# Decoder block with product-key experts, one core: searches placed among projections, normed rows remade on DVE, gathers indexed from the table

## The chip, the cores and the metric

The kernel runs on one core of a Trainium2 chip. The metric is the device time of one execution in microseconds, median of several runs, lower is better.

## The reference

One decoder block over 1024 tokens of width 1024, float32. First RMSNorm, one projection into six parts of 512, stick-breaking attention with 8 heads on three of them, a gated causal convolution of three taps on the other three; both normed, projected by `w_out` and added to x. Then the part in which the change lies, a retrieval of experts (PEER), and a last RMSNorm:

```python
xn = rmsnorm(x, ffn_norm_g)
q = (xc @ wq).reshape(128, 8, 256)                      # xc: 128 tokens of xn
s1, s2 = q[..., :128] @ keys[0], q[..., 128:] @ keys[1]   # 128 keys each
v1, i1 = top_k(s1, 16); v2, i2 = top_k(s2, 16)
cand = v1[..., :, None] + v2[..., None, :]              # 256 pairs
best, pos = top_k(cand, 16); idx = cand_idx[pos]        # of 16384 experts
g = softmax(best)
w = g * gelu(xc . u_tab[idx])
x = x + sum over heads and k of w * v_tab[idx]
```

So each of 1024 tokens reads 8 x 16 = 128 experts, and of each a row of `u` and a row of `v`, 8 KB together.

## The kernel before

**Chunks, slots, groups.** The tokens are eight chunks of 128, one token to a partition. A chunk has 128 slots, one expert of every token each. A slot is one indirect DMA of 1 MB (L758): for each partition the row of `u` and `v` beside each other, into one of eight places of `ring`. Four slots (chunks 0 and 1) or two (the others) make a group. What a group goes through:

- POOL (L742 to L760) waits until the search has found the indices (`s_exp`) and DVE has freed the first place (`s_vd`), copies the group's indices from the table `idx` into `cur_idx` (L749), waits for the copy, and then issues one gather for each slot, after DVE (`s_vd`) and PE (`s_vp`) have freed the place.
- DVE, parts 0 and 1: for each slot the dot product of the u row with the token's normed row `xn` (L1158). ACT, part 1: gelu (L797). DVE, part 2: times the gate (L1167), and then it adds the weighted v rows to `acc` (L1178). ACT, part 2: a diagonal matrix of the weights (L801). PE, part 2: diagonal times v row into PSUM, the first 512 columns (L983) and in some groups the others too (L987). In "narrow" groups PE takes two of four slots, and DVE adds the whole row of the others.
- After a chunk's last group `final_sum` (L1419, L1421) adds PSUM and `acc`; `final_root` and `final_scale` norm the result, and SP stores it.

**Fronts.** What comes before the groups of a chunk is its front: norm, projections (L1017, L1021), attention, convolution, output projection, second norm (`norm_x2`, L1279), queries (L1100), scores of the keys (L1113), the best 16 of each half (`top_keys`, L1292 to L1305) and the search: `pair_sums` and `top_pairs` (L1325 to L1350), `gate_start` (L1357 to L1369), `look_up` (L1380 to L1395) and `experts` (L1406 to L1411) on DVE, with `gate_exp` and `spread` (L928, L936) on ACT. Fronts are made for batches of chunks, [0], [1, 2], [3, 4, 5] and [6, 7]. In batch 0 a search covers two of eight heads, later four. After `norm_x2` SP stores the new x and the normed rows in DRAM (`spill`, L660 and L661), and `load_chunk` (L678, L679) loads both into `xn` and `acc` before the chunk's groups.

**The order.** `timeline()` writes out one list of groups' parts and front steps, and every engine walks through its own share of it in order. First comes the front of batch 0; once its first search is done, one part of a group follows each further step. Then a batch's front is spread by costs among the groups of the chunks before it: batch 1 among those of chunk 0, batch 2 in chunks 1 and 2, batch 3 in chunks 3 to 5. Chunks 6 and 7 have no front beside them: their first and last 8 slots are written out, the 14 bodies between run as a loop with a register. In a loop the indices' place in `idx` depends on the register.

Four searches of batch 0 stand in its query phase, one after every four lists. They use `xn` and `acc` of the other parity as room (`big`), and `ocT` for the lists (`tk`), which batch 1's front overwrites; so ACT's `store_h` of batch 1 waits for the last of them.

## Time and profile before

| | |
|---|---|
| median of 3 runs | 3197.33 us (3192.45 to 3197.36) |
| the profiled execution: own time / span | 3201.8 / 3200.1 us |
| mean granted TensorE clock | 0.863 |
| first gather / last sum of chunk 0 | 124.6 / 632 us |
| last sums of chunks 1, 2, 5, 6, 7 | 1057, 1467, 2551, 2872, 3193 us |

The profile is of one execution, in microseconds from its first instruction. Busy time is what an engine spends in instructions; a wait is the idle time before an instruction, put down to what ended last. PEclk is the granted share of TensorE's full clock. The stretches in the rows below end at the last sums of chunks.

### The profile page before, as it was taken

The numbers are of one execution on the slowest core, as the hardware profiler recorded it, in microseconds if no ns is written. First come the engines' busy times: TensorE is split into PE (matmuls) and PEld (weight loads), VectorE is DVE, ScalarE is ACT, GpSimd is POOL, SyncE is SP. The second block draws the span as 40 slices with busy tenths as digits, with TensorE's granted clock in tenths as the row PEclk, the third lists the DMA queues.
The fourth block names the chain that finished last, engine by engine and source line by source line (L and its number), as shares of the span: only waits on it lengthen the run. The fifth ranks groups of instructions, "written<-read, shape, count | busy, mean of one in ns | idle before, by whom it ended". The sixth has DMA issues, their size and how long they took to land.

```text
span 3200.1 us, 28861 instructions
## 1 busy us (share of the span) xinstructions
PE 2377.9 (74%) x7332; PEld 1255.1 (39%) x7332; DVE 2499.8 (78%) x5544; ACT 996.5 (31%) x2273; POOL 1526.3 (48%) x1488
## 2 busy tenths in 40 slices
PE   8759868588888897777787888777677756555555
PEld 7538546245545454223563444344333311111111
DVE  1676759879888789887677888879977788888887
ACT  2131521332465411234116747412122221112111
POOL 0132333333443433455444545544455567776775
PEclk9879879889999898888988989878898987777777
DMA  6879789889988999999999999999999999999998
GB/s 244 312 296 385 292 344 397 337 331 402 374 333 323 373 419 338 351 382 380 419 419 396 380 356 406 388 420 412 381 397 407 418 422 422 422 422 422 422 422 346
DMA packets 184026, 1209.11 MB, mean 378 GB/s; under 512 B 20560, under 2 KB 20560, under 8 KB 52432
## 3 DMA queue, kind: packets, MB, share of 16 engines
q0 software_dynamic: 147456, 1073.81, 83.1%
q1 hardware_dynamic: 36432, 133.73, 10.9%
q8 instruction: 55, 0.90, 0.1%
q14 instruction: 83, 0.68, 0.1%
HBM read 1194.87 MB, written 12.58 MB: 377 GB/s over the span
## 4 chain that ended last, share of the span: by engine, by line
DVE 32%; DMA 26%; PE 23%; ACT 11%; issue 6%; POOL 2%; POOLq 0%; DVEq 0%; SPq 0%; ACTq 0%
DMA ring<-in_uv,cur_idx 24%; DVE ring L1158 13%; PE vacc L983 8%; DVE acc L1178 7%; PE bank L1021 5%; ACT L776 3%; PE bank L1089 3%; POOL ring L758 2%; ACT g_ge L797 2%; ACT diag L801 1%; PE bank L1017 1%; PE o_ps L987 1%; DVE lt L1295 1%; DMA xn_scratch<-xb 1%; DVE g_w L1167 1%
## 5 line engine op out<-in xcount | busy, mean ns | idle before, releaser
L983 PE MATMUL vacc<-ring,diag 128*128 128x512 f32 x1872 | 1180.7, 759 | 751.7 <-ACT diag L801 751.5
L758 POOL DMA_INDIRECT ring<-in_uv,cur_idx x1024 | 1197.2, 1169 | 1017.3 <-PE vacc L983 459.3
L1158 DVE CUSTOM_DVE_ANT_0 ring<-ring,xn 128x1024 f32<-128x1024 f32 x1024 | 1229.5, 1221 | 246.8 <-DMA ring<-in_uv,cur_idx 244.4
L983 PEld LDWEIGHTS vacc<-ring,diag 128*128 128x128 f32 x1872 | 395.6, 229 | 1404.9 <-ACT diag L801 1054.1
L1178 DVE SCALAR_TENSOR_TENSOR acc<-ring,g_w,acc 128x512 f32<-128x512 f32 (+1 forms) x854 | 689.1, 807 | 40.5 <-DVE g_w L1167 0.3
L749 POOL COPY cur_idx<-idx 128x2 uint32<-128x2 uint32 (+2 forms) x448 | 327.2, 730 | 631.5 <-DVE acc L1178 489.6
L797 ACT ACTIVATE g_ge<-dots 128x2 f32<-128x2 f32 (+1 forms) x448 | 91.2, 204 | 1656.2 <-DVE dots L1158 1655.5
L801 ACT ACTIVATE diag<-ident,g_w 128x128 f32<-128x128 f32 x936 | 322.1, 393 | 124.3 <-DVE g_w L1167 124.2
L1021 PE MATMUL bank<-hT,wpool 128*128 128x256 f32 (+2 forms) x1280 | 289.8, 385 | 3.3 <-ACT hT L831 3.3
L1021 PEld LDWEIGHTS bank<-hT,wpool 128*128 128x128 f32 x1280 | 223.6, 196 | 78.1 <-issue 19.5
L776 ACT ACT_TABLE_LOAD x187 | 239.9, 1283 | 4.1 <-PEq L1447 0.8
L1100 PE MATMUL bank<-hT,wpool 128*128 128x256 f32 (+2 forms) x1024 | 240.0, 391 | 1.4 <-ACT hT L913 1.4
L1167 DVE TENSOR_TENSOR g_w<-g_ge,gate 128x2 f32<-128x2 f32 (+1 forms) x448 | 72.0, 161 | 200.8 <-ACT g_ge L797 200.6
L1100 PEld LDWEIGHTS bank<-hT,wpool 128*128 128x128 f32 x1024 | 180.5, 200 | 47.8 <-issue 3.4
L987 PE MATMUL o_ps<-ring,diag 128*128 128x512 f32 x340 | 193.0, 652 | 0.0
L987 PEld LDWEIGHTS o_ps<-ring,diag 128*128 128x128 f32 x340 | 72.1, 212 | 95.4 <-issue 95.4
L1032 PEld LDWEIGHTS bank<-qT,kT 64*128 64x128 f32 x576 | 71.0, 194 | 50.9 <-issue 43.3
L1032 PE MATMUL bank<-qT,kT 64*128 64x128 f32 x576 | 84.0, 291 | 1.2 <-ACT ab L882 1.2
L1158 DVE DVE_READ_ACCUMULATOR2_ANT dots<- 128x1 f32 x1024 | 84.9, 83 | 0.0
L1066 PEld LDWEIGHTS o_ps<-ab,vN 128*64 128x64 f32 x576 | 61.9, 138 | 45.0 <-issue 41.2
L1066 PE MATMUL o_ps<-ab,vN 128*64 128x128 f32 x576 | 78.7, 282 | 0.0
L1050 PE MATMUL bank<-lb,neg_tri 128*128 128x512 f32 x144 | 78.4, 627 | 0.0
(143 smaller groups left out, 1602.6 us busy)
## 6 DMA issues: line engine op xcount, KB each, us to landing
wpool<-in_w_in SPq DMA_DIRECT2D x96, 512.0 KB, 7.9
wpool<-in_peer_wq SPq DMA_DIRECT2D x64, 512.0 KB, 8.7
wpool<-in_w_out SPq DMA_DIRECT2D x32, 512.0 KB, 7.9
ring<-in_uv,cur_idx POOLq DMA_INDIRECT x1024, 11.6
xb<-in_x SPq DMA_DIRECT2D x15, 512.0 KB, 8.3
x_scratch<-xb SPq DMA_DIRECT2D x8, 512.0 KB, 10.1
xn_scratch<-xb SPq DMA_DIRECT2D x8, 512.0 KB, 12.5
xn<-xn_scratch SPq DMA_DIRECT2D x8, 512.0 KB, 8.5
```

The lines of the kernel that those rows point to most:

```text
L749: nc.gpsimd.tensor_copy(cur_idx[:, sl], idx[:, c % KEEP, bass.ds(i * RING + q * group_of(c), group_of(c))])\
L758: nc.gpsimd.indirect_dma_start(ring[:, s, :], None, uv, bass.IndirectOffsetOnAxis(ap=cur_idx[:, s:s + 1], axis=0))\
L776: nc.scalar.preload_act_table_set(name)
L797: nc.scalar.activation(g_ge[:, sl], dots[:, sl], ACT.Gelu_apprx_tanh).then_inc(s_gge, 1)
L801: nc.scalar.activation(diag[:, q * group_of(c) + s, :], ident[:, :], ACT.Copy, scale=g_w[:, q * group_of(c) + s:q * group_of(c) + s + 1]). ...
L983: ins = nc.tensor.matmul(vacc[:, :], diag[:, q * group_of(c) + s, :], ring[:, q * group_of(c) + s, D:D + PE_COLS], start=first and s == 0, ...
L987: ins = nc.tensor.matmul(o_ps[:, :], diag[:, q * group_of(c) + s, :], ring[:, q * group_of(c) + s, D + PE_COLS:2 * D], start=first_wide an ...
L1021: ins = nc.tensor.matmul(b[:, 0:T], w[:, k * P:(k + 1) * P], hT[:, k, 0:T], start=k == 0, stop=k == KD - 1)
L1032: ins = nc.tensor.matmul(b[:, i * P:(i + 1) * P], kT[rows, i, kb * P:(kb + 1) * P], qT[rows, i, span(c)], start=i == 0, stop=False, skip_g ...
L1100: ins = nc.tensor.matmul(b[:, 0:T], w[:, k * P:(k + 1) * P], hT[:, k, 0:T], start=k == 0, stop=k == KD - 1)
L1158: ins = nc.vector.tensor_tensor_reduce(out=ring[:, s, 0:D], in0=ring[:, s, 0:D], in1=xn[:, c % 2, :], scale=1.0, scalar=0.0, op0=ALU.mult, ...
L1178: nc.vector.scalar_tensor_tensor(out=acc[:, c % 2, lo:D], in0=ring[:, s, D + lo:2 * D], scalar=g_w[:, s:s + 1], in1=acc[:, c % 2, lo:D], o ...
```

## The change

**Searches.** In batch 0's query phase only the first search stays. `own_places` puts the other three into chunk 0's groups: for heads 2, 4 and 6 the pairs go behind part 2 of groups 3, 5 and 7, `gate_start` behind part 0 of the next group, `look_up` behind its part 2, and `experts` behind part 0 of the group after it. The lists of chunk 0 move from `ocT` to `lists_own`, and `store_h` of batch 1 no longer waits for the searches. Batch 1's front begins after group 2 instead of group 3.

**Normed rows.** `spill` stores only x, `load_chunk` loads only `acc`, and a new step `norm_chunk` on DVE makes the chunk's normed rows in `xn` from `acc`, the row's root (now kept per chunk in `root2`) and the gain. `load_chunk` 0 moves ahead of the first query; `norm_chunk` stands after the first search for chunk 0, and for the others near the end of the chunk before.

**Indices.** In written-out groups the gather takes its indices from a column of `idx`, and POOL copies none; it waits for `s_exp`, and for each slot for `s_vd` and `s_vp`. In loops the copy stays.

```diff
-        if bi == 0 and (t + 1) % (2 * hs) == 0:
-            search(at, k + 4, chunks[0], t // 2 + 1 - hs)
+        if bi == 0 and t + 1 == 2 * hs:
+            search(at, k + 4, chunks[0], 0)
...
+def own_places():
+    hs, places = heads_per_search(0), {}
+    for h in range(hs, PH, hs):
+        g = OWN_FIRST + h - hs
+        for i, step in enumerate(own_search(h)):
+            places.setdefault((g + (i + 1) // 2, 0 if i % 2 else 2), []).append(step)
+    return places
...
     for step in front_steps(0):
+        if ("pe", "query", 0, 0) in step:
+            out.append(("front", "sp", "load_chunk", 0))
...
                 if not known:
-                    out.append(("front", "sp", "load_chunk", 0))
+                    out.append(("front", "dve", "norm_chunk", 0))
...
                     out.append(("group", c, g, part))
+                    if c == 0:
+                        for step in own.pop((g, part), []):
+                            out += phases(step)
...
+                if g == groups_of(c) * 31 // 32:
+                    out.append(("front", "dve", "norm_chunk", c + 1))
...
-                    sp.dma_start(xn_d[c], xb[:, 1, :]).then_inc(s_spx, 16)
...
-                    sp.wait_ge(s_spx, 32 * (c + 1))
-                    sp.dma_start(xn[:, c % 2, :], xn_d[c]).then_inc(s_chunk[c % 2], 16)
+                    sp.wait_ge(s_spx, 16 * (c + 1))
                     sp.dma_start(acc[:, c % 2, :], x2_d[c]).then_inc(s_chunk[c % 2], 16)
...
-                if not very_first:
+                copied = not isinstance(i, int)
+                if copied:
                     pool.wait_ge(s_vd, used + 1)
-                sl = slice(q * group_of(c), (q + 1) * group_of(c))
-                nc.gpsimd.tensor_copy(cur_idx[:, sl], idx[:, c % KEEP, bass.ds(i * RING + q * group_of(c), group_of(c))])\
-                    .then_inc(s_idx, 1)
-                pool.wait_ge(s_idx, group_no(c, i, q) + 1)
+                    sl = slice(q * group_of(c), (q + 1) * group_of(c))
+                    nc.gpsimd.tensor_copy(cur_idx[:, sl],
+                                          idx[:, c % KEEP, bass.ds(i * RING + q * group_of(c), group_of(c))])\
+                        .then_inc(s_idx, 1)
+                    pool.wait_ge(s_idx, copies(c, i, q) + 1)
...
-                    nc.gpsimd.indirect_dma_start(ring[:, s, :], None, uv,
-                                                 bass.IndirectOffsetOnAxis(ap=cur_idx[:, s:s + 1], axis=0))\
+                    row = cur_idx[:, s:s + 1] if copied else idx[:, c % KEEP, i * RING + s:i * RING + s + 1]
+                    nc.gpsimd.indirect_dma_start(ring[:, s, :], None, uv, bass.IndirectOffsetOnAxis(ap=row, axis=0))\
                         .then_inc(s_gat[s], 16)
...
-                    if bi > 0:
+                    if bi > 1:
                         act.wait_ge(s_exp, found([e for e in BATCHES[bi - 1] if e not in LATE][-1], PH - 1))
...
                     if c >= KEEP:
-                        dve.wait_ge(s_idx, groups_ahead(c - KEEP + 1))
+                        dve.wait_ge(s_fsum, c - KEEP + 1)
...
+                elif name == "norm_chunk":
+                    c, = args
+                    dve.wait_ge(s_chunk[c % 2], 16 * (c // 2 + 1))
+                    if c == 1:
+                        dve.wait_ge(s_exp, found(0, PH - 1))
+                    if c >= 2:
+                        dve.wait_ge(s_fsq, c - 1)
+                    nc.vector.scalar_tensor_tensor(out=xn[:, c % 2, :], in0=acc[:, c % 2, :], scalar=root2[:, c:c + 1],
+                                                   in1=ffn_gain[:, :], op0=ALU.mult, op1=ALU.mult).then_inc(s_xnc, 1)
```

How the order moves, at three places. DVE in the query phase, from the end of the first search, before (the names are output<-inputs; `ocT` and `bank` rows are a step of `top_keys`):

```order
L1411 TENSOR_TENSOR gate<-srch,gs 128x32
L1325 TENSOR_TENSOR xn<-ocT 128x2x128
L1326 TENSOR_TENSOR xn<-ocT 128x2x8
L1337 MAX srch<-xn 128x8 x2
L1340 MATCH_REPLACE acc<-srch,xn 128x136 x2
L1344 MAX_INDEX srch<-srch,xn 128x8 x2
L1347 MAX srch<-acc 128x8 x2
L1350 MAX_INDEX srch<-srch,acc 128x8 x2
L1292 MAX ocT<-bank 128x8
```

and in the changed kernel, whose line numbers stand 41 higher here:

```order
L1452 TENSOR_TENSOR gate<-srch,gs 128x32
L1333 MAX lists_own<-bank 128x8
L1336 MATCH_REPLACE lt<-lists_own,bank 128x128
L1340 MAX_INDEX lists_own<-lists_own,bank 128x8
L1343 MAX lists_own<-lt 128x8
L1346 MAX_INDEX lists_own<-lists_own,lt 128x8
L1462 SCALAR_TENSOR_TENSOR xn<-acc,root,ffn_gain 128x1024
```

The pairs of the second search are gone from here; the lists follow at once, and `norm_chunk` 0 after one list.

DVE in the changed kernel at groups 4 and 5, where batch 1's projections run (ISA rows are dot products):

```order
L1208 TENSOR_TENSOR g_w<-g_ge,gate 128x4
L1219 SCALAR_TENSOR_TENSOR acc<-ring,g_w,acc 128x512 x4
L1421 TENSOR_TENSOR xn<-acc,iota 128x1024
L1425 TENSOR_TENSOR acc<-xn,srch 128x1024
L1432 TENSOR_TENSOR xn<-acc 128x512
L1432 TENSOR_TENSOR acc<-xn 128x256
L1432 TENSOR_TENSOR xn<-acc 128x128
L1436 TENSOR_TENSOR srch<-xn 128x64
L1199 ISA ring,dots<-ring,xn 128x1024
```

The look-up of the second search now stands between group 4's additions and group 5's dot products.

POOL from the first gather on, with the semaphores it waits for, before:

```order
L749 COPY cur_idx<-idx 128x4 [waits s_exp]
L758 DMA ring<-in_uv,cur_idx 128x2048 [waits s_idx]
L758 DMA ring<-in_uv,cur_idx 128x2048 x3
L749 COPY cur_idx<-idx 128x4 [waits s_exp]
L758 DMA ring<-in_uv,cur_idx 128x2048 [waits s_idx]
L758 DMA ring<-in_uv,cur_idx 128x2048 x3
L749 COPY cur_idx<-idx 128x4 [waits s_vd,s_exp]
L758 DMA ring<-in_uv,cur_idx 128x2048 [waits s_idx,s_vd,s_vp]
L758 DMA ring<-in_uv,cur_idx 128x2048 [waits s_vd,s_vp] x3
```

and changed:

```order
L800 DMA ring<-in_uv,idx 128x2048 [waits s_exp]
L800 DMA ring<-in_uv,idx 128x2048 x3
L800 DMA ring<-in_uv,idx 128x2048 [waits s_exp]
L800 DMA ring<-in_uv,idx 128x2048 x3
L800 DMA ring<-in_uv,idx 128x2048 [waits s_exp,s_vd,s_vp]
L800 DMA ring<-in_uv,idx 128x2048 [waits s_vd,s_vp] x3
```

The copies and the waits for them are gone; the first gather of a group waits for both engines itself.

## Rows read from the trace of the kernel before

**Rows 1.** The page: busy time of each engine (share of the span) x instructions.
```profile
PE 2377.9 (74%) x7332; PEld 1255.1 (39%) x7332; DVE 2499.8 (78%) x5544; ACT 996.5 (31%) x2273; POOL 1526.3 (48%) x1488
```

**Rows 2.** Busy time by stretch: us, engines (x instructions), PEclk, DMA share, GB/s.
```profile
222.00:305.00 83.00, 82.45 (x416) 69.81 (x417) 51.80 (x87) 12.06 (x37) 26.57 (x28) 1.00 0.98 387
...
222.00:632.00 410.00, 335.67 (x1307) 224.47 (x1308) 304.22 (x744) 113.76 (x240) 141.23 (x136) 0.90 0.90 352
...
124.00:1467.00 1343.00, 1061.98 (x3618) 611.81 (x3616) 1092.49 (x2688) 445.01 (x918) 532.04 (x523) 0.89 0.91 356
1467.00:2551.00 1084.00, 842.47 (x2468) 436.21 (x2468) 851.86 (x1819) 398.71 (x888) 544.92 (x576) 0.88 0.98 399
2551.00:2872.00 321.00, 182.73 (x256) 57.24 (x256) 260.10 (x451) 61.65 (x198) 228.58 (x192) 0.77 1.01 422
```

**Rows 3.** Waits (us in total, times, longest): 124 to 1467 us, then 1467 to 2551.
```profile
POOL ring L758 <- PE vacc L983: 231.1, 81, 12.8
...
DVE ring L1158 <- DMA ring<-in_uv,cur_idx: 75.6, 45, 5.1
...
DVE ring L1158 <- DMA ring<-in_uv,cur_idx: 121.9, 109, 3.1
```

**Rows 4.** DVE in order of time, 152 to 173 us: start, us, operation.
```profile
152.75 0.18 DVE L1406 TENSOR_REDUCE gs<-srch 128x2 f32<-128x32 f32 x1
...
153.46 0.42 DVE L1325 TENSOR_TENSOR xn<-ocT 128x256 f32<-128x256 f32 x1
...
156.84 0.30 DVE L1292 MAX8 ocT<-bank 128x8 f32<-128x128 f32 x1
...
169.66 0.68 DVE L1380 TENSOR_TENSOR xn<-acc,iota 128x1024 bf16<-128x1024 bf16 x1
...
172.41 0.30 DVE L1292 MAX8 ocT<-bank 128x8 f32<-128x128 f32 x1
```

**Rows 5.** DVE, ACT and PE in order of time, from 134.99 us.
```profile
134.99 1.22 DVE L1158 CUSTOM_DVE_ANT_0 ring<-ring,xn 128x1024 f32<-128x1024 f32 x1 [5.08 <-DMA ring<-in_uv,cur_idx]
...
197.53 1.06 ACT L816 ACTIVATE xb<-xb 128x1024 f32<-128x1024 f32 x1
...
209.38 1.06 ACT L816 ACTIVATE xb<-xb 128x1024 f32<-128x1024 f32 x1 [4.96 <-DMA xb<-in_x]
...
214.47 5.30 PE L983 MATMUL vacc<-ring,diag 128*128 128x512 f32 x8 [11.91 <-ACT diag L801]
```

**Rows 6.** The page: costliest groups, DVE's dot products and additions.
```profile
L1158 DVE CUSTOM_DVE_ANT_0 ring<-ring,xn 128x1024 f32<-128x1024 f32 x1024 | 1229.5, 1221 | 246.8 <-DMA ring<-in_uv,cur_idx 244.4
...
L1178 DVE SCALAR_TENSOR_TENSOR acc<-ring,g_w,acc 128x512 f32<-128x512 f32 (+1 forms) x854 | 689.1, 807 | 40.5 <-DVE g_w L1167 0.3
```

**Rows 7.** PE in order of time, 222 us: the first projection of batch 1.
```profile
222.55 2.64 PE L1021 MATMUL bank<-hT,wpool 128*128 128x256 f32 x11 [1.91 <-ACT hT L831]
```

**Rows 8.** POOL in order of time, 1240 us: copy and the two gathers behind it.
```profile
1240.34 0.69 POOL L749 COPY cur_idx<-idx 128x2 uint32<-128x2 uint32 x1 [0.43 <-DVE acc L1178]
1241.97 0.96 POOL L758 DMA_INDIRECT ring<-in_uv,cur_idx  x1 [0.93 <-PE vacc L983]
1243.24 0.94 POOL L758 DMA_INDIRECT ring<-in_uv,cur_idx  x1 [0.30 <-issue]
```

**Rows 9.** Copies and gathers on POOL: duration ns min/median/max.
```profile
L749 POOL COPY cur_idx<-idx x448: 182/691/1284, 123.5 to 3170.9; 128x2 uint32<-128x2 uint32 x91, 128x2 uint32 x37, 128x4 uint32<-128x4 uint32 x22
...
L758 POOL DMA_INDIRECT ring<-in_uv,cur_idx x1024: 932/1010/1999, 124.6 to 3174.8; - x171
```

**Rows 10.** The page: DMA issues x count, KB each, median us to landing.
```profile
x_scratch<-xb SPq DMA_DIRECT2D x8, 512.0 KB, 10.1
xn_scratch<-xb SPq DMA_DIRECT2D x8, 512.0 KB, 12.5
xn<-xn_scratch SPq DMA_DIRECT2D x8, 512.0 KB, 8.5
```

**Rows 11.** The multiplication that makes the normed rows: duration ns min/median/max.
```profile
L1279 DVE SCALAR_TENSOR_TENSOR xb<-xb,st,ffn_gain x8: 1279/1280/1284, 91.3 to 2089.0; 128x1024 f32<-128x1024 f32 x8
```

More of the change, by code:

```diff
@@ L43 @@
 EARLY_PARTS = 1
+OWN_FIRST = 3
 PARTS = 3
@@ L200, in front_steps, with own_search, at @@
     return [steps[i] for i in sorted(steps)]
+def own_search(h):
+    steps = {}
+    def at(k, eng, *phase):
+        steps.setdefault(k, []).append((eng, *phase))
+    search(at, 0, 0, h)
+    return [steps[i] for i in sorted(steps)]
+def own_places():
[5 more added lines that the diff above has]
+    return places
 COST = {"gate_h": 0.9, "conv_taps": 1.6, "att_soft": 0.8, "att_carry": 0.6, "gain_mix": 1.2, "add_mix": 1.3,
@@ L452, in build @@
         st = sb("st", [P, 16])
+        root2 = sb("root2", [P, CHUNKS])
         dots = sb("dots", [P, RING])
@@ L584, in diags_ahead, with copies @@
             return slot_no(c, i, q) - sum(group_of(e[0]) // 2 for e in narrow if e < (c, g))
+        looped = [c for kind, c, first, count in (ph for ph in line if ph[0] == "body") if count > 1]
+        def copies(c, i, q):
+            ahead = sum((BODIES - 2) * lap_of(k) for k in looped[:looped.index(c)])
+            return (i - 1) * lap_of(c) + (ahead + q)
         def gather_line(eng_group, eng_front, me):
```

20 lines of the change are left out of this document (12 added, 8 removed).

## The prediction, made before the changed kernel ran

> **What bounds the kernel now.** I read the page first, for the shares of the engines [rows 1]: DVE is busy 78% of the span, PE 74%. No engine is full over the whole span, so the page alone doesn't tell what bounds it. The busy time by stretch does [rows 2]. In the last two chunks, where only loops run, DMA moves 422 GB/s at a share of 1.01 while DVE has a fifth of its time free: bytes bound that part, and I take 422 GB/s as what DMA can give. From 1467 to 2551 us it is 399 GB/s at a share of 0.98, almost as full. From 124 to 1467 us it is 356 GB/s at 0.91, with DVE busy 1092.5 of 1343 us. There nothing is full; the stretch is bound by latency, by engines that work in order and wait for one another. So a saved wait can pay before 1467 us, and after it mainly saved bytes. Then I read the waits, to see what of DVE's idle time hangs on gathers: 75.6 us in 45 waits before 1467 us and 121.9 us in 109 waits after it [rows 3]. The rest of DVE's idle time hangs on PE and ACT.
>
> **Step 1, own searches (-13 us).** The change takes the last three searches of chunk 0 out of the query phase and puts them among batch 1's projections. One such search costs DVE 0.71 us for the experts, 3.38 us for pair sums and top pairs (152.75 to 153.46 to 156.84), and 2.75 us for the look-up (169.66 to 172.41) [rows 4]; the start of the gates is as many small operations as the experts, so another 0.7. That is 7.5 us, and 22.5 us for three. None of it goes away; the question is where it stands.
>
> How much sooner do the projections begin? The first dot product waits for its gather until 134.99, and batch 1's first norm starts on ACT at 197.53 [rows 5]. Of the DVE work between the two, the change takes out 22.5 us of searches, except the 3.4 us of pairs that already ran before 134.99, so 19; and it takes out one group of four slots (turn_h(1) now follows group 2, it followed group 3), four dot products of 1.22 us and four additions of 0.75 to 0.81 us, about 8 us [rows 6]. DVE is nearly full there, so the norm starts 27 us sooner. The second norm keeps its 11.85 us behind the first (its x has to be loaded). In the trace of before, its transposes then stand behind group 4's product, 5.30 us on PE [rows 5]; in the new order they stand ahead of group 3's. So the projections start not 27 but 32 us sooner, at about 190 instead of 222.55 [rows 7].
>
> What has to be done afterwards is more, by the same searches and one group. The searches fall into the projections, where PE is busy 82.45 of 83 us at full clock and DVE 51.8 [rows 2]: 31 us free for 22.5 us of searches, though not always at the right moment. I let 4 us of them through. The one group costs what a group costs in the rest of this stage: 410 us for 26 to 27 groups, 15 us. So 32 - 15 - 4 = 13 us gained. The ends: if the additional 30.5 us of DVE work is done at DVE's present share of that stage (304.22 of 410, 0.74 [rows 2]) it takes 41 us, 9 us more than the head start; if all of it finds a gap, the whole 32 us stay. I take 13 because the projections, the nearest rows, have the gap in the very place.
>
> **Step 2, POOL's copies (-18 us).** 336 of the 448 copies go; the 112 in the loops stay. A copy takes 0.69 us and the gather behind it starts 0.93 us after its end, where gathers behind each other stand 0.30 us apart [rows 8]: a group's gathers can leave 0.69 + 0.93 - 0.30 = 1.32 us earlier if the copy is what they wait for. Often it isn't: the copy waits only for DVE, the gather also for PE's product, and where PE is last (230 us of POOL's waits before 1467 us name it, [rows 3]) the copy is hidden already. What an earlier gather is worth is bounded by the waits of DVE for gathers. Before 1467 us: 45 waits of at most 1.32 us, 59 us; at the low end nothing, if PE is last each time. I take a fifth, 12 us, since many of the 45 also wait behind weights in the DMA queues. From 1467 to 2551 us, DMA's share leaves 2% of 1084 us, 22 us [rows 2]; I take 6. Together 18, between 0 and 81.
>
> Here a rule speaks against a part of this. The copy takes 182 ns at its fastest and 691 in the median [rows 9], and it mostly starts as DVE's first addition of a group ends and the second, which reads two operands from SBUF, begins. The gather too varies, from 932 to 1999 ns [rows 9]. 
>
> **Step 3, no normed rows in DRAM (-10 us).** Eight stores and eight loads of 512 KB go [rows 10], 8.4 MB, at 422 GB/s 20 us. That is the far end; the near end is 0, if they all lie where DMA has room. They are spread over all stages; the ones behind 1467 us lie where DMA is at a share of 0.98 and more [rows 2], so I take half, 10. In it is a shorter wait for the spill: the store of the normed rows lands 12.5 us after its issue in the median, and the next x, the squares and the keys wait for it. SP now waits for the spill of chunk 0 (a median of 10.1 us to landing) before it issues the last eight weight tiles of the queries; the tiles are prefetched eight deep, and DVE, which takes the results, is behind by then. I cost it at nothing; uncovered it would be at most those 10 us.
>
> **Step 4, remaking them (+4 us).** DVE gets eight multiplications of 128x1024, as long as the ones that make the rows today, 1.28 us [rows 11], 10.2 us in all. The load of each is issued several groups before, so none should wait. Three are in the stages before 1467 us, where DVE's work is paid: 4 us. The others lie where DMA is full and cost nothing (at the far end all 10). Two more table loads on ACT, and lists of chunk 0 in another buffer, I cost at nothing: ACT is busy 31% [rows 1].
>
> **Sum.** -13 - 18 - 10 + 4 = -37 us. The profiled execution took 3201.8 us around a span of 3200.1; it stands 4.5 us above the median of the runs, 3197.33. So 3165 for such an execution and 3160 us against the median.
>
> **The rivals.**
> (a) *DMA sets the pace anyway.* Waits saved before 1467 us are lost again at the chunk's ends, and only bytes count: 5 to 10 us, about 3190. For it: shares of 0.9 and more nearly everywhere. Against it: 356 GB/s instead of 422 in the first 1343 us. Chance 0.14; half of it lies within 0.2%, which is 6 us and about what a measurement of this kernel can tell from no change.
> (b) *The wait for DVE passes to the gather.* Of the 1.32 us, 0.69 - 0.18 = 0.51 go back; step 2 gives 18 x 0.81 / 1.32 = 11 us, and the time is 3167. For it: the 691 against 182 ns. Against it: gathers behind DVE's additions also come at 0.93 us. Chance 0.12.
> (c) *The copies and idle gaps pay fully.* Steps 1 and 2 near their far ends, -28 and -40, step 3 -15, step 4 +4: 3118. For it: every chunk before 1467 us is a chain of waits. Chance 0.14.
> (d) *Slower: the searches stop the projections.* DVE works in order; a search between two parts of a group holds the dot products, then ACT's gelu, then PE's products, which stand in PE's queue ahead of the next projection. It decides against the change as soon as less than about half of the searches finds a gap while the head start is spent. Price +9 us by the far end of step 1 and +10 of step 4; if at the same time PE is last for every gather (step 2 gives 0) and bytes give 5: 3197 + 14 = 3211. Chance 0.09. Against it: 31 us free on DVE in the projections.
> My forecast, 3140 to 3180, has the remaining 0.51.
>
> **How the numbers follow.** The time is that of the forecast, 3160. The range reaches up to rival (a), 3193, and down to (c), 3118; outside lie (d) and pieces of (a) and (c), some 0.2. Faster by over 0.2%: 0.51 + 0.12 + 0.14 + half of (a) = 0.84; within 0.2%: 0.08 with a little of (d); slower 0.08.
>
> **What would show it.** Right: the first projection (L1021 with 128x256) at about 190 us, chunk 0's last sum some 13 to 30 us sooner than 632; DVE's share in the projections up from 0.62 to near 0.9; no copy before 2550 us; gathers 0.30 us behind each other also at a group's start, of 0.93 to 1.2 us each; DMA 8.4 MB less, its rate before 1467 us up from 356 GB/s; the last two chunks at 321 us as now. Wrong: first projection later than 200; PE idle between projections with DVE in a search; gathers at a group's start of 1.5 us and more (b); every stage shorter only by its bytes (a); a wait of DVE for the rows of a chunk.

## The result, and the profile after

The changed kernel takes 3168.05 us (median of 4 runs, 3166.28 to 3171.32) where the kernel before, measured beside it, takes 3196.52 (4 runs, 3192.45 to 3197.36): a ratio of 0.9914, 95% interval 0.9898 to 0.9931. That is 28 us faster. The forecast was 37 us faster, 3160, with a range of 3118 to 3193.

The profiled execution took 3166.99 us around a span of 3164.9; before it was 3201.8 around 3200.1. So the profiled pair shows some 7 us more than the medians do, and every difference between single profiles below carries a few us of that kind.

The page of the changed kernel, busy time and DMA packets [rows 1 and 10 answer to it]:

```profile
PE 2361.8 (75%) x7332; PEld 1248.4 (39%) x7332; DVE 2507.5 (79%) x5552; ACT 998.0 (32%) x2275; POOL 1337.3 (42%) x1152
...
DMA packets 181717, 1200.68 MB, mean 379 GB/s; under 512 B 20304, under 2 KB 20304, under 8 KB 50128
```

1200.68 MB are 8.4 MB less than before, as the forecast's third step said. DVE has 8 us more work than before (2507.5 us, it had 2499.8 [rows 1]) and 35 us less to do it in.

Where the time went shows in the end of each chunk (us from the span's start), read from the records of both traces as the start of DVE's last sum, which adds PE's columns from `vacc` to `acc`:

| chunk | 0 | 1 | 2 | 3 | 4 | 5 | 6 | 7 |
|---|---|---|---|---|---|---|---|---|
| before, end | 632 | 1057 | 1467 | 1841 | 2213 | 2551 | 2872 | 3193 |
| after, end | 603 | 1029 | 1438 | 1811 | 2181 | 2519 | 2838 | 3158 |
| before, length | 632.1 | 424.8 | 409.8 | 374.1 | 371.9 | 338.6 | 321.2 | 320.8 |
| after, length | 603.3 | 425.4 | 409.7 | 372.4 | 370.2 | 337.7 | 319.3 | 320.2 |

28.8 us are gone by the end of chunk 0, and 6.3 in the seven chunks after it. Some of the 28.8 is the profiled execution of before being late there: in four kernels below that leave the searches where they were and differ from before in other things (idx_only, split_waits, store_kept, two_copies) chunk 0 ends at 625 to 629. So 22 to 26 us are nearer to what the change takes off chunk 0. The same stretches as in [rows 2], bounded by the chunks' new ends (columns: us, engines busy with their instructions, granted clock as a share of 2.4 GHz, DMA share, GB/s):

```profile
190.00:273.00 83.00, 83.00 (x396) 67.92 (x395) 71.16 (x191) 22.44 (x48) 27.27 (x22) 0.99 0.94 369
...
222.00:603.00 381.00, 310.52 (x1178) 200.92 (x1177) 312.06 (x798) 116.32 (x239) 126.17 (x107) 0.89 0.90 360
124.00:1438.00 1314.00, 1052.23 (x3621) 605.42 (x3619) 1095.47 (x2691) 445.39 (x919) 454.15 (x391) 0.90 0.91 360
1438.00:2519.00 1081.00, 836.32 (x2468) 435.50 (x2468) 856.13 (x1824) 399.81 (x889) 442.38 (x385) 0.89 0.98 398
2519.00:2838.00 319.00, 181.65 (x256) 56.67 (x256) 260.58 (x452) 61.63 (x198) 221.70 (x184) 0.76 1.01 422
```

The first line is the stretch of batch 1's projections. PE is as full as before, and DVE is busy 71.16 of 83 us where it was busy 51.80 [rows 2]. The last three lines are shorter than those of [rows 2] by 29, 3 and 2 us, and apart from POOL's the engines' busy times are nearly the same: before chunk 3 the rate is 360 GB/s instead of 356, from there to chunk 5's end 398 instead of 399. POOL is busy 78 us less before 1438 us, and 103 us less from there to 2519. What that did to the gathers the next views show.

The head start, in the order of time of ACT and of PE (start, us, operation, in brackets the idle time before it and its releaser, that is, what ended last before it); the answers to [rows 5] and [rows 7]:

```profile
170.09 1.06 ACT L857 ACTIVATE xb<-xb 128x1024 f32<-128x1024 f32 x1
```

PE in order of time, from the second norm's transposes to the first projection:

```profile
185.22 1.72 PE L1043 MATMUL bank<-ident,xb 128*128 128x128 f32 x8 [4.66 <-ACT xb L860]
189.08 5.31 PE L1024 MATMUL vacc<-ring,diag 128*128 128x512 f32 x8 [2.15 <-ACT diag L842]
194.22 5.99 PE L1062 MATMUL bank<-hT,wpool 128*128 128x256 f32 x27
```

The norm of batch 1 starts at 170.09 instead of 197.53 us, 27.4 sooner; the first projection at 194.22 instead of 222.55, 28.3 sooner. The second norm came at 182.22, 12.1 us behind the first. Its transposes do stand ahead of a group's product now, at 185.22, but group 3's product (5.31 us) still stands between them and the first projection.

The waits that the second step hung on, before chunk 2's end (us in total, times, longest); [rows 3] answers:

```profile
DVE ring L1199 <- DMA ring<-in_uv,idx: 70.3, 45, 5.9
```

And from there to chunk 5's end:

```profile
DVE ring L1199 <- DMA ring<-in_uv,idx: 116.4, 105, 2.6
```

DVE waited for gathers 75.6 us in 45 waits before and waits 70.3 in 45 now; behind chunk 2 it was 121.9 us in 109, now 116.4 in 105. The copies' removal was to shrink these.

How a gather at a group's start stands to PE, in rows of PE and of POOL. They answer to [rows 8]. PE's product of two slots (four matmuls) there begins at 1239.91:

```profile
1239.91 1.98 PE L983 MATMUL vacc<-ring,diag 128*128 128x512 f32 x4 [2.31 <-ACT diag L801]
```

Its second matmul, the one that frees the first place, ends at 1241.03, and the copy ends at 1241.03 too. The gather starts at 1241.97, 2.06 us behind the product's start. Then the changed kernel, PE, DVE and POOL together:

```profile
1206.65 1.91 PE L1024 MATMUL vacc<-ring,diag 128*128 128x512 f32 x4
...
1207.57 1.22 DVE L1199 CUSTOM_DVE_ANT_0 ring<-ring,xn 128x1024 f32<-128x1024 f32 x1
...
1208.50 1.10 POOL L800 DMA_INDIRECT ring<-in_uv,idx  x1 [5.39 <-PE vacc L1024]
...
1210.86 1.98 PE L1024 MATMUL vacc<-ring,diag 128*128 128x512 f32 x4 [2.31 <-ACT diag L842]
...
1212.79 0.94 POOL L800 DMA_INDIRECT ring<-in_uv,idx  x1 [1.95 <-PE vacc L1024]
```

Without a copy the gather comes 1.85 and 1.93 us after the product's start, with the copy 2.06. In these groups the copy costs 0.1 to 0.2 us and not 1.32, since the gather waits for the product in both kernels.

How it is over all groups can be read from the records of both traces. In both kernels the first gather of a group never starts sooner than 0.80 us behind the end of the matmul that frees its place; in the changed kernel it starts just then in most groups, and in the kernel before in half of them. In the latter no first gather starts sooner than 0.93 us behind the end of its copy either. So one can ask for each of the 318 groups of chunks 0 to 5 that wait for a place how much later the first gather left than PE and the gather before it allow:

| first gathers of a group that left late: how many, us in all | before | changed | idx_only | two_copies |
|---|---|---|---|---|
| chunks 0 to 2, of 126 groups | 49, 25 | 3, 4 | 3, 4 | 73, 70 |
| chunks 3 to 5, of 192 groups | 101, 67 | 6, 6 | 6, 6 | 149, 169 |

(idx_only and two_copies are experiments below: the kernel before without the copies, and with a second one.) Before, 150 of 318 first gathers left late, by 0.59 us in the median and 92 us in all, and 138 of them started within 0.96 us behind their copy. Without copies it is 9, by 9 us. So the copies cost the gathers 82 us in all; three quarters of that lie in chunks 3 to 5, where DMA's share is 0.98.

### The profile page after: what moved, and what is told of

Same layout as the page of the kernel before. It is cut to its first block, busy times and chain, and to the rows that moved or that the text cites. A ratio compares the mean times of both kernels' runs of the same rounds, so it can differ in the third digit from the quotient of the medians.

```text
span 3164.9 us, 28192 instructions
## 1 busy us (share of the span) xinstructions
PE 2361.8 (75%) x7332; PEld 1248.4 (39%) x7332; DVE 2507.5 (79%) x5552; ACT 998.0 (32%) x2275; POOL 1337.3 (42%) x1152
## 2 busy tenths in 40 slices
DMA packets 181717, 1200.68 MB, mean 379 GB/s; under 512 B 20304, under 2 KB 20304, under 8 KB 50128
## 4 chain that ended last, share of the span: by engine, by line
DVE 30%; DMA 28%; PE 23%; ACT 11%; issue 6%; POOL 2%; POOLq 0%; DVEq 0%; ACTq 0%; SPq 0%
DMA ring<-in_uv,idx 15%; DVE ring L1199 13%; DMA ring<-in_uv,cur_idx 11%; PE vacc L1024 9%; DVE acc L1219 7%; PE bank L1062 5%; ACT L817 4%; PE bank L1130 3%; ACT g_ge L838 1%; ACT diag L842 1%; POOL ring L800 1%; PE bank L1058 1%; DVE lt L1336 1%; DVE g_w L1208 1%; DMA x_scratch<-xb 1%
## 5 line engine op out<-in xcount | busy, mean ns | idle before, releaser
L800 POOL DMA_INDIRECT ring<-in_uv,idx x800 | 927.2, 1159 | 1646.5 <-PE vacc L1024 854.7
L800 POOL DMA_INDIRECT ring<-in_uv,cur_idx x224 | 286.4, 1279 | 145.0 <-POOL cur_idx L789 80.1
L789 POOL COPY cur_idx<-idx 128x2 uint32 x112 | 121.7, 1087 | 11.8 <-DVE acc L1219 11.2
```

The lines of the kernel that those rows point to most:

```text
L800: nc.gpsimd.indirect_dma_start(ring[:, s, :], None, uv, bass.IndirectOffsetOnAxis(ap=row, axis=0))\
```

## The experiments

All 12 kernels have medians beside the kernel before, on the same chip; its medians there were 3195.88 to 3197.74 us. First the three parts of the change, each alone, and the change without one of them.

### Own searches alone: own_only

The kernel before with the three searches of chunk 0 moved among batch 1's projections, their lists in a buffer of their own and ACT's `store_h` of batch 1 no longer waiting for them, and nothing else. What the dropped wait is worth without the move wasn't measured.

```diff
+OWN_FIRST = 3
-        if bi == 0 and (t + 1) % (2 * hs) == 0:
-            search(at, k + 4, chunks[0], t // 2 + 1 - hs)
+        if bi == 0 and t + 1 == 2 * hs:
+            search(at, k + 4, chunks[0], 0)
+    own = own_places()
                     out.append(("group", c, g, part))
+                    if c == 0:
+                        for step in own.pop((g, part), []):
+                            out += phases(step)
```

> The kernel before with the searches moved and nothing else: POOL's copies and the normed rows in DRAM stay. Theory O (the gain is that of the searches; in the changed kernel chunk 0's stage ends 28.8 us sooner and the seven others together only 6.3): chunk 0's last sum at 603 to 608 us instead of 632, ratio to before 0.991 to 0.993. Theory C (searches bring the 13 us that the prediction gave them, the copies the other 15 in chunk 0): last sum at 617 to 621, ratio 0.995 to 0.997.

Measured: 3179.66 us (3173.36 to 3184.39, 6 runs) beside 3197.6, ratio 0.9941 (0.9921 to 0.996): 18 us. Chunk 0 ends at 607 instead of 632 (or of 625 to 629, above). This part carries most of the gain. By the interval it is 13 to 25 us, so the forecast's 13 lies at its lower end. The ratio lies between those of the two theories and is clear of neither; the stage's end fits theory O.

### Indices straight from the table alone: idx_only

```diff
-                nc.gpsimd.tensor_copy(cur_idx[:, sl], idx...)\
-                    .then_inc(s_idx, 1)
-                pool.wait_ge(s_idx, group_no(c, i, q) + 1)
+                copied = not isinstance(i, int)
+                if copied:
...
+                    row = cur_idx[:, s:s + 1] if copied else idx[:, c % KEEP, i * RING + s:i * RING + s + 1]
```

> The kernel before with gathers that take their indices from the table in written-out groups, and nothing else. Theory O: nothing, ratio 0.999 to 1.001, every stage within 2 us, since a gather waits for PE's product or starts 0.9 us after its release with and without a copy. Theory C: chunk 0's last sum 10 to 15 us sooner, ratio 0.993 to 0.997.

Measured: 3196.65 us (3190.67 to 3202.98, 12 runs) beside 3197.6, ratio 0.9996 (0.9983 to 1.0008). The 320 copies of chunks 0 to 5 are gone and the time doesn't move. The stages of its profiled execution, the fastest of the twelve, aren't all within 2 us of before (chunk 0 ends at 625, chunk 4 takes 366 us instead of 372), so theory O holds for the time and not for every stage. A first view of why is what released the gathers. The trace of the kernel before, POOL's idle time ahead of its gathers from 124 to 2551 us, by releaser (us in total, times):

```profile
L758 POOL DMA_INDIRECT ring<-in_uv,cur_idx x775: 932/962/1999, 124.6 to 2549.7; - x194
its engine sat idle before it (us, times) until:
  PE vacc L983: 426.7, 203
  issue: 180.9, 419
  PE o_ps L987: 101.3, 47
  DVE acc L1178: 79.8, 45
  POOL cur_idx L749: 38.0, 41
```

And idx_only in the same stretch:

```profile
  PE vacc L992: 846.4, 206
  DVE acc L1187: 286.7, 47
  PE o_ps L996: 186.6, 74
```

Before, the view names the copy 41 times and PE 250 times (203 and 47). Without copies PE is named 280 times and DVE 47, and their idle times are longer by what the copy had cut out of them. But the 41 is too low a count of the groups that a copy held up. The view names whatever ended last before the gather, and that is often PE's product for the next place, not for the one that this gather takes. Measured from the matmul that frees the place, it was some 140 groups (table above).

So the gathers did leave sooner in idx_only, by 82 us in all, and the kernel's time doesn't show it: the gain is 1 us, by the interval between 5 us faster and 3 slower. What is known of the reason is where the 82 us lie, 61 of them in chunks 3 to 5, in which DMA has 2% of its time free, and 21 in chunks 0 to 2. DVE's waits for gathers from 124 to 2551 us were 197.5 us before and are 193.2 here. Why 21 us of sooner gathers in the first chunks bring nothing that can be seen, no run shows.

### Normed rows remade alone: norm_only

```diff
-                    sp.dma_start(xn_d[c], xb[:, 1, :]).then_inc(s_spx, 16)
-                    sp.dma_start(xn[:, c % 2, :], xn_d[c]).then_inc(s_chunk[c % 2], 16)
+                elif name == "norm_chunk":
...
+                    nc.vector.scalar_tensor_tensor(out=xn[:, c % 2, :], in0=acc[:, c % 2, :], scalar=root2[:, c:c + 1],
+                                                   in1=ffn_gain[:, :], op0=ALU.mult, op1=ALU.mult).then_inc(s_xnc, 1)
```

> The kernel before with the normed rows remade on DVE and not stored, and nothing else. Theory O: only the bytes count, and only where DMA is full (chunks 2 to 7, some 12 of 16 transfers of 1.3 us at most): ratio 0.997 to 0.999. Rival: DVE's 10 us cancel them, ratio 0.9995 to 1.002, with chunks 0 to 2 slower by 1.3 us each.

Measured: 3186.66 us (3180.63 to 3191.32, 11 runs) beside 3197.6, ratio 0.9968 (0.9956 to 0.9979): 11 us. Steps 3 and 4 together were forecast at 6, and theory O's range is just missed on the fast side.

### The change with the copies put back: own_norm

```diff
-                copied = not isinstance(i, int)
-                if copied:
+                if not very_first:
...
+                                                  bass.IndirectOffsetOnAxis(ap=cur_idx[:, s:s + 1], axis=0))\
```

> The changed kernel with POOL's copies back in every group. Theory O: as fast as the changed kernel, ratio to before 0.990 to 0.993, chunk 0's last sum at 603 to 606. Theory C: chunk 0's last sum at 613 or later and ratio 0.994 or more.

Measured: 3172.31 us (3168.7 to 3174.76, 6 runs) beside 3197.6, ratio 0.9921 (0.9904 to 0.9938): 25 us, where the change has 28 (0.9914, 0.9898 to 0.9931). The two intervals overlap almost wholly. The ratio is theory O's; chunk 0 ends at 608, between the two theories' places. The parts add up within their spread: 18 and 11 are 29, beside 25 for both together. The copies are worth 1 us by idx_only and 3 by this pair, where 18 were forecast; neither is clear of zero.

### A second copy for each group: two_copies

If taking a copy away gives nothing, does a second one cost anything? The kernel before with one more copy ahead of the first, waited for.

```diff
+                if isinstance(i, int):
+                    more[0] += 1
+                    nc.gpsimd.tensor_copy(spare_idx[:, sl], idx...).then_inc(s_idx2, 1)
+                    pool.wait_ge(s_idx2, more[0])
                 nc.gpsimd.tensor_copy(cur_idx[:, sl], idx...)
```

> The kernel before with a second copy of a group's indices on POOL ahead of the first one, waited for, in the written-out groups: some 1.6 us more between DVE's release and the gather. Theory H (one copy is hidden because PE's product ends later than the copy, by little): the two no longer fit, a gather leaves about 1.5 us later in most groups, and chunks 0 to 5 lose part of it: ratio 1.002 to 1.02. Rival (gathers' departure has slack everywhere in these stages): 1.000 to 1.002.

Measured: 3203.63 us (3195.26 to 3207.19, 12 runs) beside 3197.74, ratio 1.002 (1.0008 to 1.0033): 6 us slower. POOL in order of time shows two groups. In both the gather starts 0.93 us behind the second copy's end, though the view names PE in one of them:

```profile
1253.38 0.69 POOL L755 COPY spare_idx<-idx 128x2 uint32<-128x2 uint32 x1 [3.82 <-DVE acc L1187]
1254.13 0.18 POOL L758 COPY cur_idx<-idx 128x2 uint32<-128x2 uint32 x1
1255.24 0.96 POOL L767 DMA_INDIRECT ring<-in_uv,cur_idx  x1 [0.93 <-PE vacc L992]
...
1261.49 0.69 POOL L755 COPY spare_idx<-idx 128x2 uint32<-128x2 uint32 x1 [4.04 <-DVE acc L1187]
1262.24 1.07 POOL L758 COPY cur_idx<-idx 128x2 uint32<-128x2 uint32 x1
1264.25 0.96 POOL L767 DMA_INDIRECT ring<-in_uv,cur_idx  x1 [0.93 <-POOL cur_idx L758]
```

By the table above 222 of 318 groups now leave later than PE allows, instead of 150, by 240 us in all instead of 92. (The view by releasers has 111 gathers named with a copy, instead of 41, and is too low in the same way.) So 148 us of later gathers cost 6 us, by the interval 3 to 11. Theory H expected 1.5 us more in most groups, and the mean is 0.5. At the same price the first copy's 82 us would be worth 3 us, which idx_only's interval and own_norm's 3 us allow. Whether the first copy costs nothing or those few us can't be told; that it costs 18 can be excluded.

### Which part of the moved searches pays: own_old_places and searches_apart

own_only does two things. It takes searches out of the time before the first projections and puts them into it; and the front steps of batch 1 start one group earlier. own_old_places keeps the first and undoes the second.

```diff
+    while early < 11:
+        out.append(("group", 0, *chunk0[early]))
+        early += 1
     own = own_places()
```

> own_only with batch 1's front started where the kernel before starts it (behind part 1 of group 3), so that every front step stands behind the same group part as before, and only the three searches are elsewhere. In own_only chunk 0 gains 8 us at group 5 and again 12 us between groups 17 and 18, where the kernel before stands 27 us. Theory G (the searches in the projections' gaps are the gain): this kernel keeps both parts, chunk 0's last sum at 605 to 612, ratio to before 0.993 to 0.996. Theory P (the second part is one of places: in own_only the output projection of chunk 2 stands elsewhere between the groups when its x is late): group 18's interval stays 25 to 27 us, last sum at 618 to 626, ratio 0.996 to 0.998.

Measured: 3181.15 us (3172.18 to 3190.2, 6 runs) beside 3197.74, ratio 0.9955 (0.9943 to 0.9967): 17 us, beside own_only's 18. The profiled execution was the fastest of the six, so its stages flatter it. The earlier front shows no worth of its own here; what pays is where the searches stand. The first projection came at 207.65 us:

```profile
207.65 7.17 PE L1051 MATMUL bank<-hT,wpool 128*128 128x256 f32 x32 [1.88 <-ACT hT L861]
```

That is 11.8 us later than own_only's 195.81, and yet the end is the same within the spread; more of the groups stand ahead of the front and are done by then. Here a head start of the projections and groups already done trade one for one (early_five, below, gets more out of a head start than this).

searches_apart moves the three searches of the changed kernel to the groups 3, 9 and 15, so that the later two stand behind the projections.

```diff
-        g = OWN_FIRST + h - hs
+        g = OWN_FIRST + (h - hs) * 3
```

> The changed kernel with its three searches behind groups 3, 9 and 15 instead of 3, 5 and 7: two of them in the attention, where DVE is fuller and PE emptier. Theory G (the gaps of the projections hide them): chunk 0's last sum 5 to 12 us later than 603, ratio to before 0.9935 to 0.996. Theory P: within 3 us of 603, ratio 0.990 to 0.993.

Measured: 3173.29 us (3167.24 to 3176.52, 5 runs) beside 3197.74, ratio 0.9922 (0.9909 to 0.9935); the change has 3168.05. Chunk 0 ends at 613 instead of 603. Its projections, 190 to 273 us:

```profile
190.00:273.00 83.00, 83.00 (x398) 68.02 (x397) 59.37 (x123) 14.24 (x38) 25.95 (x22) 0.99 0.95 370
```

DVE is busy 59.37 us here, and 71.16 in the changed kernel. Two searches that miss this gap cost some 5 us by the medians and 10 by the profiled chunk 0; 15 us of DVE work was moved. That would put the gap's worth at a third to two thirds of the work put in it. But the intervals of the two ratios overlap widely: chunk 0's end fits theory G, the ratio fits theory P, and the cost of the other places isn't proved.

### Bytes or waits in the remade rows: split_waits and store_kept

The kernel before had one semaphore for both stores of a spill, so the load of the next x waited for the second store too, without need. split_waits gives the second store a semaphore of its own and keeps all bytes.

```diff
+        s_spn = sem("s_spn")
-                    sp.dma_start(xn_d[c], xb[:, 1, :]).then_inc(s_spx, 16)
+                    sp.dma_start(xn_d[c], xb[:, 1, :]).then_inc(s_spn, 16)
...
-                        act.wait_ge(s_spx, 32 * c)
+                        act.wait_ge(s_spn, 16 * c)
```

> The kernel before with a semaphore of its own for the store of the normed rows: the next load of x waits only for the store of x, the next squares only for the store of the normed rows; both stores and both loads stay, all bytes too. Theory W (remaking the rows gains by the wait behind the second store, which ends 12.0 us after its issue where the store of x alone ends 8.7 us after): group 18 comes 2 to 8 us sooner as in norm_only (8.4), ratio 0.997 to 0.999. Theory B (it gains by its bytes): nothing, 0.9995 to 1.0005.

Measured: 3197.8 us (3191.67 to 3210.37, 12 runs) beside 3197.74, ratio 1.0003 (0.9992 to 1.0014). The load of x was issued 8.2 us behind the store instead of 12.1, and nothing came of it.

store_kept is norm_only (rows remade, none loaded) with the store of the normed rows put back, read by nobody.

```diff
                     sp.dma_start(x2_d[c], xb[:, 0, :]).then_inc(s_spx, 16)
+                    sp.dma_start(xn_d[c], xb[:, 1, :]).then_inc(s_spn, 16)
```

> The kernel before with the remade normed rows, and with the store of the normed rows to DRAM put back (its load is not): the rows in DRAM are read by nobody, the square of the next chunk waits for it with a semaphore of its own, the next x load for the store of x alone. norm_only took 10.9 us off (3186.66 beside 3197.6), split_waits (waits parted, bytes kept) nothing. Theory bytes of the store (4 MB that pass on the DMA rings in the stretch in which x_scratch is stored and x is loaded again, chunk 0's group 18 among it): nearly all of norm_only's gain is gone, 3194 to 3199, and the 27 us between groups 17 and 18 stay over 22. Theory load (the 4 MB read again, at the start of each chunk, are what counted) or theory wait: the gain stays, 3185 to 3190.

Measured: 3193.06 us (3186.99 to 3208.39, 12 runs) beside 3195.88, ratio 0.9989 (0.9974 to 1.0004). Of norm_only's 11 us about 3 are left, and these are not clear of zero. So dropping the load, with the remaking on DVE paid, was worth little, and dropping the store some 8, between the two theories and nearer to that of the store's bytes. The two ratios are 0.0021 apart and their intervals just touch, so the 8 is rough. ACT's wait for the last store, in the spill of chunk 1 (395 to 440 us; us in total, times, longest), shows one way in which it costs. The kernel before:

```profile
ACT xb L890 <- DMA xn_scratch<-xb: 7.7, 1, 7.7
```

norm_only:

```profile
ACT xb L895 <- DMA x_scratch<-xb: 4.0, 1, 4.0
```

store_kept:

```profile
ACT xb L900 <- DMA xn_scratch<-xb: 7.5, 1, 7.5
```

`square_mix` on ACT overwrites the normed rows, so it waits until they are stored. Between the `g_w` steps of groups 17 and 18 of chunk 0, where this spill lies, the kernels need 26.8 us (before), 22.0 (split_waits), 22.1 (store_kept) and 18.2 (norm_only). The step from 22 to 18 may be that wait's 3.5 us; the one from 26.8 to 22 isn't a result of any of the edits, as idx_only, which doesn't touch the spill, has 22.2 as well. Chunk 0 of the profiled execution of before was slow in this place. That is where some of the profiled pair's 35 us, against 28 by the medians, may come from.

### Could it be better: early_five, own_four, five_and_four

The groups ahead of the front of batch 1 are limited to five parts instead of what the finished searches allow, so that the front begins sooner; or the searches of chunk 0 stand one group later, behind groups 4, 6 and 8 instead of 3, 5 and 7 (the text on own_four below names other groups).

```diff
-                if chunk0[early][0] < known:
+                if chunk0[early][0] < known and early < 5:
```
```diff
-OWN_FIRST = 3
+OWN_FIRST = 4
```

> The changed kernel with at most five parts of chunk 0's groups written ahead of the front steps of batch 1, so that they begin sooner. Theory A (the gaps of the first projections are the only place in chunk 0 where DVE's searches hide; everything before them is paced by the DMA rings and by the norm of batch 1): the norm of batch 1 at ACT at 160 or sooner instead of 170, the first projection 5 to 10 us sooner than 194, time 3160 to 3166 beside 3168.05. Rival B (gathers pause while the front steps come first, the pause is not made good): 3168 to 3175.

> The changed kernel with each search of batch 1 one group later (behind groups 4, 5, 6 and not 3, 4, 5). Theory A (a search costs nothing as long as it lies in the projections' stretch, 190 to 273 us): within 3 us of 3168.05, chunk 0 ends at 601 to 607. Rival B (the place behind group 3 is just where DVE waits, one later runs into the sums of groups): 3172 to 3176, chunk 0 ends at 608 or later.

> The changed kernel with both moves: at most five parts ahead of the front steps of batch 1, and each search one group later. early_five measured 3160.38 us, own_four 3166.64 beside 3168.05 for the change. Theory (the two gains are separate and real): 3157 to 3161, under early_five's median. Rival (own_four's 1.4 us is the spread between executions, early_five's 7.7 is real): 3160 to 3164, same as early_five within its spread. Rival (early_five's median is luck as well, as its profiled execution shows chunk 0 ending at 604 beside 603): 3165 to 3170.

Measured: early_five 3160.38 us (3157.84 to 3162.44, 4 runs) beside 3195.88, ratio 0.9883 (0.9859 to 0.9906); own_four 3166.64 (3164.56 to 3168.93, 4 runs), ratio 0.9901 (0.9878 to 0.9924); both edits 3160.86 (3156.31 to 3167.37, 5 runs) beside 3196.72, ratio 0.9892 (0.9878 to 0.9906). The changed kernel had 3168.05, 0.9914 (0.9898 to 0.9931), beside other runs of before. The ratios' intervals overlap, so the 7 us between it and early_five aren't proved, but two kernels with that edit came out at the same 3160 to 3161. own_four can't be told from the change. early_five's PE in order of time:

```profile
185.43 7.17 PE L1062 MATMUL bank<-hT,wpool 128*128 128x256 f32 x32 [1.89 <-ACT hT L872]
192.44 3.60 PE L1024 MATMUL vacc<-ring,diag 128*128 128x512 f32 x8
```

The first projection is 8.8 us sooner than in the changed kernel, with the product that stood ahead of it (189.08 above) now behind it. That speaks against the one-for-one trade of own_old_places; the spread of that kernel's six runs, 18 us, leaves room for both. Where the 7 us show up isn't settled: in the profiled executions chunk 0 ends at 604 in early_five and at 596 in five_and_four beside 603, and early_five's chunk 4 takes 365.6 us beside 370.2, a difference that own_norm (367.2) and own_old_places (366.0) show as well, though their edits don't touch that chunk. early_five is the best version found: faster than before by 1.2% (0.9 to 1.4).

## Why the prediction was right, and where it was wrong

**What bounds the kernel.** Right as far as it went. The last two chunks stay at 422 GB/s and about 320 us, as forecast. From chunk 3 to 5 DMA's share of 0.98 stayed, and no gain from POOL can be seen there, though 61 of the 67 us by which first gathers were late there are gone. "Latency" before 1467 us was too coarse a word: it didn't say whose.

**Step 1, own searches, -13.** The mechanism was right and the size came out too small: own_only gained 18 us (13 to 25). The norm was forecast 27 us sooner and came 27.4 sooner. The projections were forecast 32 sooner, at 190, and came 28.3 sooner, at 194.22, since I read the order as if group 3's product had moved behind the first projection; it hadn't. That term was 4 us too good. "I let 4 us of them through" and "the one group costs 15 us" were then too dear. With 28 us of head start and 18 of gain, the two together cost 10 us, not 19. own_old_places suggests why the second hurts so little: with the groups ahead put back to their old number the time was the same within the spread (17 us gained), so a group that stands behind the front's start costs about what it gives. DVE's share in the projections went from 0.62 to 0.86, near the 0.9 named. Putting two searches elsewhere (searches_apart) cost 5 us, which isn't clear of the spread.

**Step 2, POOL's copies, -18.** Wrong. idx_only gave 1 us, within its interval nothing, and the change with the copies back lost 3 of 28, with intervals that overlap. Two readings failed. The first is the size of what a copy holds up: "a group's gathers can leave 0.69 + 0.93 - 0.30 = 1.32 us earlier if the copy is what they wait for". PE's product was there almost as late. The copy held up some 140 of 318 groups, and all copies together 82 us: 0.26 us for a group in the mean. In [rows 8] itself it was 0.13 us, with PE's matmul and the copy both ending at 1241.03; most of the 0.93 us behind the copy is also there behind a matmul (0.80 us at 1208.50 and 1212.79 above, without a copy).

The second and larger one is the worth of a sooner gather. The forecast took a fifth of 45 waits of 1.32 us before chunk 2's end, and 6 us behind it, from DVE's waits for gathers [rows 3]. The gathers left 82 us sooner in all in idx_only, and neither the time nor DVE's waits moved with it (75.6 to 70.3 and 121.9 to 116.4 in the changed kernel). From chunk 3 on this is where DMA was read as nearly full, and the 6 us there had no other ground than the 2% left. For the first three chunks the cause stays open.

**Rival (b), the wait for DVE passes to the gather.** Its time, 3167, is nearly the measured one; that is luck, since 0.51 us did not pass. The median over all gathers of chunks 0 to 5 fell from 962 to 938 ns:

```profile
L800 POOL DMA_INDIRECT ring<-in_uv,idx x776: 932/938/2139, 124.7 to 2518.8; - x194
```

That of a group's first gather, which the copy stood before, rose from 1.00 to 1.09 us, its mean from 1.18 to 1.19. All 768 gathers of chunks 0 to 5 together take 13 us more than before (887.6 and 874.6 us); 0.51 us for each of 320 groups would be 163. But the wait that (b) builds on is real, for gathers as well as for copies, and was there before the change. The 0.69 us of a copy that begins beside DVE's additions is what the rule of the Trainium skill, page "SBUF — State Buffer", section "SBUF: two separate sides", would have. This case's traces agree: in the kernel before, 374 copies began while DVE was in a dot product or an addition, which both read two operands from SBUF, and all 374 ended within 0.1 us of its end; the other 74 took 0.19 us in the median. How gathers wait is in the section on the hardware.

**Steps 3 and 4, the rows, -10 and +4.** norm_only gained 11 us where the two steps had 6. The sum was too small by 5. "Half of 20 us of bytes" was the wrong way to price it. store_kept, which drops the 4.2 MB of loads and remakes the rows, gained 3, and dropping the 4.2 MB of stores some 8 more, though at 422 GB/s they are only 10 us and by the same half would be 5. The stores lie in front of steps that wait for them; of "a shorter wait for the spill" ACT's part may count (7.5 to 4.0 us in one spill), as parting SP's wait gave nothing (split_waits). What else of the 8 is bytes and what is ACT's wait wasn't parted. Remaking the rows on DVE wasn't measured alone; `norm_chunk` takes 1.27 us, as long as forecast.

**The sum.** -13 - 18 - 6 were forecast, and -18, -1 and -11 measured for the parts alone, -28 for all. Half of the forecast's 37 us hung on step 2, which is nearly empty; two terms that came out 5 us too small each made good a part of it. So 3160 against 3168 is luck in good part, and closer than the working deserves. Rival (a), "only bytes count", falls with own_only; (c), that copies pay fully, with idx_only; (d), searches that stop the projections, with DVE's 71.16 us in PE's full 83.00.

## What to carry to other kernels

Before a removed instruction is given a price, measure how much later its successor starts than its other conditions allow, in each case and from the very event that it needs. The list of releasers is a first look and can mislead, since it names what ended last and not what was needed: here it had 41 where some 140 were held up. Then ask what a sooner start is worth, above all where DMA is nearly full: 82 us of sooner gathers gave 1 us. Work of an engine is best moved into a stretch in which another engine is full and this one isn't: here three searches of 7.5 us, put where PE was busy 83 of 83 us, gained 18 us. When a store is dropped, look at who overwrites what it reads: that wait, and not only the bytes, goes with it (here 3.5 us at one spill; its share in the gain wasn't measured).

## What the runs showed of the hardware

The way from the PE matmul that frees a place to the start of a gather on POOL took 0.80 us at the least, in the kernel before and in the changed one, and the way from the end of a copy on POOL 0.93 us. The very first gather of the changed kernel, which waits for DVE's `gate` alone, started 0.95 us after it ended. Gathers issued behind each other stood 0.30 us apart in the median. Taking the copies away shortened none of these.

Instructions on POOL were held up by what DVE did beside them, the issue of a gather too. In the kernel before, 331 gathers of chunks 0 to 5 began at least 0.1 us before the end of a dot product or an addition on DVE. 320 of them ended 0.79 to 0.88 us after that DVE instruction's end, however early they had begun, and so took up to 2.0 us, 1.32 in the median; the other 437 took 0.94 us in the median. In the changed kernel it is 336 of 353. The gather at 1208.50 above is one: the dot product ends at 1208.79, the gather at 1209.60. Copies of 128x2 elements show the same in two_copies, where POOL's second copy took 0.18 us in one group and 1.07 in the next (1262.24 to 1263.31, above). DVE beside the latter:

```profile
1260.60 1.54 DVE L1187 SCALAR_TENSOR_TENSOR acc<-ring,g_w,acc 128x512 f32<-128x512 f32 x2
1262.05 1.22 DVE L1167 CUSTOM_DVE_ANT_0 ring<-ring,xn 128x1024 f32<-128x1024 f32 x1
```

The first copy there began at 1261.49 beside the additions and ended with them, after 0.69 us; the second began beside the dot product and ended with it. Where the second took 0.18 us (1254.13), DVE was in `top_keys`, which reads one operand.

Executions of one kernel spread by up to 21 us when there are enough of them (before, 23 runs: 3182.96 to 3204.32), so a profiled pair alone can't decide a difference of 5.
